# Keys' sums of squares as a product with a matrix of ones, and five rotary-and-plain score products in place of six

## The reference, cut to what matters

```python
q = (rms_norm(c_q, cq_g) @ w_uq).reshape(b_, t_, MLA_HEADS, QK_HEAD)
ckv = rms_norm(c_kv, ckv_g)
k_nope = (ckv @ w_uk).reshape(b_, t_, MLA_HEADS, QK_NOPE)
v = (ckv @ w_uv).reshape(b_, t_, MLA_HEADS, V_HEAD)
k_r = jnp.broadcast_to(k_rope[:, :, None, :], (b_, t_, MLA_HEADS, QK_ROPE))
k = jnp.concatenate([k_nope, k_r], axis=-1)
q = rms_norm(q, qn_g)
k = rms_norm(k, kn_g)
q = jnp.concatenate([q[..., :QK_NOPE], apply_rope(q[..., QK_NOPE:], cos, sin)], axis=-1)
k = jnp.concatenate([k[..., :QK_NOPE], apply_rope(k[..., QK_NOPE:], cos, sin)], axis=-1)
o = causal_block_attention(q, k, v)
```

## Time and profile before

| | us |
|---|---|
| median of three runs | 1754.62 |
| lowest, highest | 1753.0, 1754.93 |
| the profiled execution | 1751.97 |
| its span, first to last instruction | 1750.2 |
| TensorE busy in it | 1734.3 (99%) |
| VectorE busy | 813.8 (46%) |
| ScalarE busy | 467.3 (27%) |
| GpSimd busy | 1183.7 (68%) |

### The profile page before, as it was taken

How to read it: one execution, slowest core, us unless ns; L and a number is a source line. 1 busy time by engine, 2 the same in 40 slices (tenths; PEclk the granted TensorE clock), 3 DMA queues, 4 the chain that set the end, 5 groups by cost and what they waited for, 6 DMA issues and landing times.

```text
span 1750.2 us, 32871 instructions
## 1 busy us (share of the span) xinstructions
PE 1734.3 (99%) x12264; PEld 1626.1 (93%) x12264; DVE 813.8 (46%) x1373; ACT 467.3 (27%) x843; POOL 1183.7 (68%) x1365
## 2 busy tenths in 40 slices
PE   7999999999999999999999999999999999999999
PEld 7999999999999999999999999989998888888887
DVE  7755546455555452212347546464555554422221
ACT  4423223242323331101134232332323233311110
POOL 7754746374798777777766647473847988777773
PEclk9999999999999999999999999999999999999999
DMA  4321212122322223222431312222222222422233
GB/s 158 123 96 54 90 59 84 65 74 70 109 84 84 84 96 130 88 96 85 161 112 64 105 56 74 72 84 68 72 77 104 85 93 86 145 88 92 96 121 110
DMA packets 47489, 161.60 MB, mean 92 GB/s; under 512 B 5408, under 2 KB 6816, under 8 KB 47136
## 3 DMA queue, kind: packets, MB, share of 16 engines
q1 hardware_dynamic: 41328, 146.56, 24.6%
q10 hardware_dynamic: 6112, 14.39, 2.2%
HBM read 152.27 MB, written 10.81 MB: 93 GB/s over the span
## 4 chain that ended last, share of the span: by engine, by line
PE 96%; DVE 2%; ACT 1%; issue 0%; ACTq 0%; DVEq 0%
PE slots L508 83%; PE slots L566 4%; PE slots L599 3%; PE slots L542 2%; PE slots L660 2%; PE slots L584 1%; PE slots L551 1%; DVE h_lo L1099 1%; DVE branch_lo L1111 1%; DVE h_tile L1175 0%; PE slots L701 0%; DVE spare L1120 0%; PE slots L569 0%; ACT cq_hi L849 0%; DVE early L1165 0%
## 5 line engine op out<-in xcount | busy, mean ns | idle before, releaser
L420 POOL TENSOR_TENSOR w_lo<-w_raw,w_hi 128x256 fp32r<-128x256 f32 x1004 | 828.4, 855 | 20.9
L415 POOL TENSOR_SCALAR w_hi<-w_raw 128x1024 fp32r<-128x1024 f32 x251 | 284.0, 1131 | 388.1 <-PE slots L508 380.7
L508 PE MATMUL slots<-h_hi,w_hi 128*128 128x264 f32 (+1 forms) x2112 | 522.8, 311 | 0.6
L508 PE MATMUL slots<-h_lo,w_hi 128*128 128x264 f32 (+1 forms) x2112 | 515.9, 308 | 0.0
L508 PE MATMUL slots<-h_hi,w_lo 128*128 128x264 f32 (+1 forms) x2112 | 515.1, 308 | 0.0
L508 PEld LDWEIGHTS slots<-h_hi,w_hi 128*128 128x128 f32 x2112 | 342.7, 188 | 22.9 <-issue 3.9
L508 PEld LDWEIGHTS slots<-h_hi,w_lo 128*128 128x128 f32 x2112 | 342.0, 188 | 19.1
L508 PEld LDWEIGHTS slots<-h_lo,w_hi 128*128 128x128 f32 x2112 | 342.0, 188 | 17.6
L508 PE MATMUL slots<-branch_hi,w_hi 128*128 128x264 f32 (+1 forms) x576 | 144.0, 313 | 9.6 <-DVE branch_lo L1111 8.9
L508 PE MATMUL slots<-branch_lo,w_hi 128*128 128x264 f32 (+1 forms) x576 | 142.8, 311 | 0.0
L508 PE MATMUL slots<-branch_hi,w_lo 128*128 128x264 f32 (+1 forms) x576 | 142.4, 311 | 0.0
(11 more groups left out here) (243 smaller groups left out, 2825.0 us busy)
## 6 DMA issues: line engine op xcount, KB each, us to landing
w_raw<-w_units SPq DMA_DIRECT2D x251, 512.0 KB, 3.2
stream<-sc_acc ACTq DMA_DIRECT2D x16, 264.0 KB, 3.0
sc_back<-stream SPq DMA_DIRECT2D x2, 2112.0 KB, 8.7
x_old<-stream SPq DMA_DIRECT2D x16, 264.0 KB, 4.4
stream<-residual_or_merged ACTq DMA_DIRECT2D x16, 264.0 KB, 2.5
ab_raw<-w_units SPq DMA_DIRECT2D x8, 512.0 KB, 4.6
residual_or_merged<-xt ACTq DMA_DIRECT2D x4, 528.0 KB, 7.6
stream<-xt ACTq DMA_DIRECT2D x1, 2112.0 KB, 10.3
```

Source lines behind the costliest of these rows:

```text
L415: pool.tensor_scalar(hi, raw, 1.0, 1.0, ALU.mult, ALU.mult).then_inc(sem("hi_part"), 1)
L420: op = pool.tensor_tensor(lo[:, cols], raw[:, cols], hi[:, cols].bitcast(F32), ALU.subtract)
L508: mm = pe.matmul(out[:, a_, 0:t1 - t0], w(k), x(k)[:, t0:t1], start=(n == 0), stop=(n == 3 * ks - 1))
```

## The change

The sums of squares of the keys no longer go through tokens on partitions. A new `spread_sum` multiplies the squares with a 128x128 matrix of ones, so the sum for each token stands on all partitions at once. DVE adds the rotary key's share (`kr_sum`, made once a layer in the same way), ACT takes the root and DVE the reciprocal, both now on 128x528 for each head. The two `spread` products, the ten diagonals and the ten `token_sums` of the keys are gone. The scaled rotary key is now written on all partitions, and `kr_hi` is no longer blank on its other half; the new tile `qr_both` holds for each head the hi part of its rotary queries on its own half and the lo part on the other half. One product of `qr_both` with `kr_hi` is then the sum of hi by hi and lo by hi, and the sixth product is left out. In CQ, the units kr and q1 change places, `stat_q` comes ahead of `rot`, and DVE's work on q1 moves behind `h_lo` of the last tile. In ATT, `rot` stands behind four steps of fill instead of ahead of it.

```diff
-FILLS = (2, 12, 5, 5, 6, 6, 7, 2, 6, 6, 7, 7, 6)
+FILLS = (4, 1, 9, 5, 5, 6, 6, 7, 2, 6, 6, 7, 7, 6)
...
+            def spread_sum(out, squares):
+
+                for a_ in range(2):
+                    mm = pe.matmul(out[:, a_, 0:HALF], ones[0:squares.shape[0], :],
+                                   squares[:, a_ * HALF:(a_ + 1) * HALF], start=True, stop=True)
+                return mm
...
-                             (qn_lo[:, h, :], kn_hi[:, h, :]), (qr_hi, kr_hi[:, h, :]),
-                             (qr_hi, kr_lo[:, h, :]), (qr_lo, kr_hi[:, h, :])]
+                             (qn_lo[:, h, :], kn_hi[:, h, :]), (qr_both[:, h, :], kr_hi[:, h, :]),
+                             (qr_both[:, h, :], kr_lo[:, h, :])]
...
-                out = free("CQ", l, 0, "stat_kr")
-                token_sums(out, [kr_sq[0:ROPE]]).then_inc(sem("cq_mm"), 1)
-
+                out = free("CQ", l, 0, "sum_kr")
+                spread_sum(out, kr_sq[0:ROPE]).then_inc(sem("cq_mm"), 1)
+                out = free("CQ", l, 0, "stat_q")
+                pe.wait_ge(*at("q_lat_summed", l, 0, 2))
+                token_sums(out, [q_lat_sq[0]]).then_inc(sem("cq_mm"), 1)
...
+                    for h in range(2):
+                        out = free("ATT", l, p, f"sum_k{h}")
+                        pe.wait_ge(*at("k_squared", l, p, h + 1))
+                        spread_sum(out, ct[h]).then_inc(sem("att_mm"), 1)
...
                     fill(FILLS[0])
+                    out = free("ATT", l, p, "rot")
+                    pe.wait_ge(*was_read("ATT", l, p, "qr"))
...
-                    pe.wait_ge(*at("qr_lo", l, p, 1))
+                    pe.wait_ge(*at("qr_lo", l, p, 2))
...
+                    for h in range(2):
+                        act.wait_ge(*was_read("ATT", l, p, f"sum_k{h}"))
+                        act.activation(ct[4 + h][:], ct[4 + h][:], ACT.Sqrt, bias=eps, scale=1.0 / QK).then_inc(
+                            sem("k_rms"), 1)
...
+                    for h in range(2):
+                        act.wait_ge(*at("kr_scaled", l, p, h + 1))
+                        act.activation(kr_hi[:, h, :], ct[4 + h][:], ACT.Copy).then_inc(sem("krp_hi"), 1)
+                    act.wait_ge(*at("qr_full", l, p, 1))
                     for h in range(2):
                         rows = slice(ROPE * h, ROPE * h + ROPE)
-                        act.activation(kr_hi[rows, h, :], spare[1][rows], ACT.Copy).then_inc(sem("krp_hi"), 1)
-                    act.wait_ge(*at("qr_full", l, p, 1))
-                    act.activation(qr_hi[:], ct[7][:], ACT.Copy).then_inc(sem("qr_hi"), 1)
+                        act.activation(qr_both[rows, h, :], ct[7][rows], ACT.Copy).then_inc(sem("qr_hi"), 1)
...
+                dve.wait_ge(*ready("CQ", l, 0, "sum_kr"))
+                dve.tensor_copy(halves(kr_sum), slot(slot_of("CQ", "sum_kr"))).then_inc(freed("CQ", "sum_kr"), 1)
...
                     for h in range(2):
-                        diagonal(ct[4 + h], k_inv, h, "k_diag")
+                        dve.wait_ge(*ready("ATT", l, p, f"sum_k{h}"))
+                        if h == 0:
+                            dve.wait_ge(*was_read("NORM", l, 0, "spread"))
+                        dve.tensor_tensor(halves(ct[4 + h][:]), slot(slot_of("ATT", f"sum_k{h}")), halves(kr_sum),
+                                          ALU.add).then_inc(freed("ATT", f"sum_k{h}"), 1)
+
+                    def k_inverse(h):
+
+                        dve.wait_ge(*at("k_rms", l, p, h + 1))
+                        dve.reciprocal(ct[4 + h][:], ct[4 + h][:]).then_inc(sem("k_rinv"), 1)
+
                     for g in range(2):
+                        k_inverse(g)
...
-                        dve.tensor_tensor(halves(ct[2 + h][:]), halves(ct[2 + h][:]), spread, ALU.mult).then_inc(
+                        dve.wait_ge(*at("k_rinv", l, p, h + 1))
+                        dve.tensor_tensor(ct[2 + h][:], ct[2 + h][:], ct[4 + h][:], ALU.mult).then_inc(
                             sem("k_full"), 1)
-                        dve.tensor_tensor(halves(spare[1][rows]), halves(kr_full[rows]), spread[rows],
-                                          ALU.mult).then_inc(freed("ATT", f"spread_k{h}"), 1)
+                        dve.wait_ge(*at("k_full", l, p, h + 1))
+                        dve.tensor_tensor(ct[4 + h][:], kr_full, ct[4 + h][:], ALU.mult).then_inc(
+                            sem("kr_scaled"), 1)
...
-                    dve.wait_ge(*at("qr_hi", l, p, 1))
-                    lo_part(qr_lo[:], ct[7][:], qr_hi[:], "qr_lo")
+                    for h in range(2):
+                        rows = slice(ROPE * h, ROPE * h + ROPE)
+                        other = slice(ROPE * (1 - h), ROPE * (1 - h) + ROPE)
+                        dve.wait_ge(*at("qr_hi", l, p, h + 1))
+                        lo_part(qr_both[other, h, :], ct[7][rows], qr_both[rows, h, :], "qr_lo")
```

More of the change, by code:

```diff
@@ L216, in build @@
         ones = sb("ones", [P, P])
-        lane_consts = sb("lane_consts", [P, 2 + 4 * NTOK])
+        lane_consts = sb("lane_consts", [P, 2 + 2 * NTOK])
         eps, zero = (lane_consts[:, n:n + 1] for n in range(2))
-        kr_stat, x_floor, x_rinv_sq, q_floor = (lane_consts[:, 2 + n * NTOK:2 + (n + 1) * NTOK] for n in range(4))
+        x_floor, q_floor = (lane_consts[:, 2 + n * NTOK:2 + (n + 1) * NTOK] for n in range(2))
         token = sb("token", [P, 16])
@@ L239, in build @@
             kn_hi, kn_lo = a("kn_hi", [P, 2, T]), a("kn_lo", [P, 2, T])
-            qr_hi, qr_lo = a("qr_hi", [P, T]), a("qr_lo", [P, T])
+            qr_both = a("qr_hi_and_lo", [P, 2, T])
             kr_hi, kr_lo = a("kr_hi", [P, 2, T]), a("kr_lo", [P, 2, T])
@@ L566, in scores @@
                         mm = pe.matmul(bank[:, 0:k1 - k0], q[:, q0:q0 + nq], k[:, k0:k1], start=(m == 0),
-                                       stop=(m == 5 and not masked))
+                                       stop=(m == 4 and not masked))
                     if masked:
@@ L692, in _ @@
                             tiles(cq_hi), tiles(cq_lo), KQ).then_inc(sem("att_mm"), 1)
-                    for h in range(2):
-                        out = free("ATT", l, p, f"spread_k{h}")
-                        spread(out, ct[4 + h], lambda t: at("k_diag", l, p, h * NTOK + t + 1)).then_inc(sem("att_mm"), 1)
-                    out = free("ATT", l, p, "rot")
-                    pe.wait_ge(*was_read("ATT", l, p, "qr"))
-                    for a_ in range(2):
-                        mm = pe.matmul(out[:, a_, 0:HALF], rotate, ct[7][:, a_ * HALF:(a_ + 1) * HALF],
-                                       start=True, stop=True)
-                    mm.then_inc(sem("att_mm"), 1)
                     filled = [0]
@@ L721, in _ @@
                     fill(FILLS[0])
+                    out = free("ATT", l, p, "rot")
+                    pe.wait_ge(*was_read("ATT", l, p, "qr"))
+                    for a_ in range(2):
+                        mm = pe.matmul(out[:, a_, 0:HALF], rotate, ct[7][:, a_ * HALF:(a_ + 1) * HALF],
+                                       start=True, stop=True)
+                    mm.then_inc(sem("att_mm"), 1)
+                    fill(FILLS[1])
                     stat = free("ATT", l, p, "stat_q")
@@ L737, in _ @@
                         scores(l, p, n // 5, n % 5)
-                        fill(FILLS[n + 2])
+                        fill(FILLS[n + 3])
                         if n == 5:
@@ L741, in _ @@
                         turn(l, p, n // 5, n % 5)
-                    fill(FILLS[12])
+                    fill(FILLS[13])
                     attend(l, p, 1)
@@ L861, in _ @@
                     h_upper(k)
-                q_latent(1)
+                if l > 0:
+                    act.wait_ge(sem("stored"), l * (16 * KT))
+                act.wait_ge(*ready("CQ", l, 0, "kr"))
+                act.activation(halves(kr_gained[:]), slot(slot_of("CQ", "kr")), ACT.Identity, bias=zero,
+                               scale=hparam(l, KR_G)).then_inc(sem("kr_gained"), 1)
+                act.activation(halves(kr_sq), slot(slot_of("CQ", "kr")), ACT.Square).then_inc(freed("CQ", "kr"), 1)
                 act.wait_ge(*at("kv_ms", l, 0, 1))
@@ L1247, in _ @@
                     other = slice(ROPE * (1 - h), ROPE * (1 - h) + ROPE)
-                    for part in (kr_hi, kr_lo):
-                        dve.memset(part[other, h, :].bitcast(F32), 0.0).then_inc(sem("kr_blank"), 1)
+                    dve.memset(kr_lo[other, h, :].bitcast(F32), 0.0).then_inc(sem("kr_blank"), 1)
                 with dve.Fori(0, PAIRS) as p:
@@ L1602 @@
         kr = w_in[:, K_ROPE:K_ROPE + ROPE]
-        units += [cols(w_in, C_KV, n) for n in range(KV)] + [cols(w_in, C_Q, n) for n in range(KQ - 1)]
-        units += [cols(np.concatenate([kr, kr], 1), 0, 0), cols(w_in, C_Q, KQ - 1)]
+        units += [cols(w_in, C_KV, n) for n in range(KV)] + [cols(w_in, C_Q, 0)]
```

(1 more changed line is left out.)

113 lines of the change are left out of this document (35 added, 78 removed), and 8 rows, old and new, of tables (SIGNALS, TILES).

## The result

The changed kernel took 1768.81 us (median of four runs, 1766.49 to 1771.25), the kernel before 1754.6 us beside it. The ratio is 1.0083, with a 95% interval of 1.0066 to 1.0100. I had predicted 1735 us and a range that ended at 1750 us.

The account below looks back on a forecast made before the run. PE, busy 99% of the span, was taken to bound the kernel. Savings of 14.3 + 12.2 = 26.5 us, less 5.6 and 1.5 of waits, gave 19.4 off 1751.97; plus 2.65 to the median, 1735 us, range 1726 to 1750.

Parts of the forecast that it names:

- The sums: PE in each pair: ten sums over tokens go, one costly change between product kinds comes; net 1.79 us, 14.3 in eight.
- The sixth product: Scores on PE: one of six equal products goes, saving one sixth of 73.5 us, 12.2 us (12.1 to 12.4).
- The gain arrived in time for `rot`: DVE's gain of the rotary queries ends at 171.0, PE wants it at 171.9: covered by 0.9 us.
- The wait at the scores: PE waits for DVE's `qr_lo` at the scores, 0.7 us a pair, 5.6 in eight; bounds none to 2.2 a pair.
- the waits slow the clock too: Rival: each pair's wait at the scores brings a half-clock stretch, adding 13.6 us: 1749 us, or 1745; chance 0.15.
- the three signs of being wrong: Reciprocal over 4 us, PE waiting at `rot` for the gain, or the granted clock falling within the pairs.
- 1.5 in my sum: CQ: `rot` no longer fills PE's wait for the sum of the queries; 0.75 us lost a layer, 1.5 in all (0 to 2.6).
- The half-clock term: Layer 1, behind CQ's wait: clock at 0.57 for four us, 1.7 us lost already before; the sum left it unchanged.
- Slower: Rival: the reciprocal makes eight passes, 4.5 us; PE waits 3.8 us a pair, 30.4 in all: 1760 us; chance 0.12.
- the 4.15 us that I had worked out: Reciprocal time on DVE from which the "Slower" rival decides: the wait eats 3.1 us a pair; 7.6 ns an element.
- No wait: Rival: PE never waits at the scores, through a cheap reciprocal or SBUF operations without traffic: 1728 to 1730 us; chance 0.22.
- The change does not save what it says: Rival: something that stays, such as weight loads, sets the distance of PE's products; 1753 to 1756 us; chance 0.06.

Follow-up runs that it names:

- e4: The changed kernel with six score products as before, so the keys' sums alone: 1753.44 us, 0.9998 of the kernel before.
- e2: The kernel before with five score products in place of six, sums over tokens as before: 1742.43 us, ratio 0.9939.
- f4: The changed kernel with four more fill steps ahead of the scores, `rot` of CQ in slot 0 and RG's first two units' slots exchanged: 1730.17 us, ratio 0.9870.
- h1: The kernel before with two idle reciprocals (528 and 352 columns) on DVE in each pair, ahead of the last lo part: 1785.69 us, ratio 1.0188.
- h2: The kernel before with two idle reciprocals (528 and 130 columns) on DVE in each pair, ahead of the last lo part: 1771.83 us, ratio 1.0104.
- f2: The changed kernel with two more fill steps ahead of the scores, taken from behind the third and fourth score product: 1748.52 us, ratio 0.9972.
- f3: The changed kernel with `rot` of CQ in slot 0 and RG's first two units' slots exchanged: 1760.95 us, 1.0042 of the kernel before.
- g3: f4 with six score products in place of five, so the keys' sums without their waits: 1737.75 us, ratio 0.9908.

## Why the prediction was wrong, point by point

**The PE side was right.** The sums: 1.79 us a pair predicted, 1.88 measured (e4). The sixth product: 12.2 predicted, 11.1 measured (e2). Both without waits: 3.32 predicted, 3.39 in the second pair (f4). The gain arrived in time for `rot`, as I had said.

**The wait at the scores was sized at 0.7 us and is 2.6: the step that failed.** Count from the pair's start, 153.72 in my sum and 157.31 in the trace. PE ended its fill at 30.7 (187.65 + 0.40), predicted 30.9. The gain of the rotary queries ended at 18.0 (175.33), predicted 17.3: from start to start the two reciprocals took 3.37 and 3.36 us and not 2.9, 0.9 in all, the additions took 0.2 more, and some 0.4 came back at the two `qn_lo` and the gain. The four multiplications ended at 23.0 (180.29), predicted 21.3: another 1.0, as they took 5.0 and not 4.0. The last lo part ended at 33.0 (190.34), predicted 31.5. So DVE was 1.5 later, PE 0.2 earlier, and the hand-over took 0.34 (190.34 to 190.68) where I had 0.1: 1.9 us, the difference of 0.7 and 2.6. My upper bound was 2.2 us a pair, so the bounds missed as well, by little.

The group of the reciprocal (count, busy us, mean ns, idle before):

```profile
L1266 DVE RECIPROCAL early<-early 128x528 f32<-128x528 f32 x16 | 55.2, 3448 | 1.0
L1284 DVE TENSOR_TENSOR early<-early 128x528 f32<-128x528 f32 x16 | 19.7, 1234 | 0.0
L1287 DVE TENSOR_TENSOR early<-residual_or_merged,early 128x528 f32<-128x528 f32 x16 | 20.5, 1279 | 0.6
```

The slope from ten elements to 528 is (3448 - 202) / 518 = 6.3 ns; h1 has 6.25 between 352 and 528 columns (2.35 and 3.45 us), and 130 columns in h2 took 0.97 us, on the same line. The small rows had 4.2 to 5.7: a slope over ten elements is a poor guide to one over 500. The Trainium skill, "VectorE: DVE Perf Modes", section "First, the fixed hardware budget", gives the repeat count of 8 that I had read as eight passes; the measured time is below the 4.4 us which that makes (I had written 4.5 for 8 x 1.0 x 528 ns + 0.14 us). For the multiplications I had the right row, 1.26 us beside POOL, and took 1.0 because POOL has pauses; they ran at 1.23 and 1.28 on average, so the dear end was the price.

**Even the right wait would not have given the time.** 21.0 in place of 5.6 is 15.4 us, that is 1751 us. The other 18 have three causes. (1) The clock: the rival "the waits slow the clock too" was right in kind. I gave it 0.15 with a wait of 0.7 us; at 2.6 us it happens, so one of the three signs of being wrong that I had named, a fall of the granted clock within the pairs, came true, though the reciprocal stayed under 4 us. The runs price it at 8.9 us in the pairs (the changed kernel beside f2; 7.4 to 10 by the other two ways), and h1 shows it apart from the change. (2) The end of CQ and of attention: L648 with 3.2 and L1378 with 1.9 us, and the half clock behind them; the same two slots were worth 7.9 us in f3 and 8.8 in f4, against 1.5 in my sum. That 1.5 was for another wait, the one for the sum of the queries, which `rot` no longer covers; it grew from 1.0 to 1.7 us, 0.7 in all. For the two new ones I had looked at the order on PE and not at the slot table: `rot` now takes the slot that DVE's last new pass frees, and `av1` the one that RG wants first. (3) The gap of 3.6 us at L666, which no view of the kernel before could show; 1.1 of it went in f3 and is in the 7.9. Together 15.4 + 8.9 + (7.9 - 1.5) + 2.5 = 33.2 us over 1735.3, that is 1768.5; measured are 1768.8. The fit is closer than the terms are known: each is a difference of medians with an interval of some 3 us, and those across chips move by 1.5 us with the runs of the kernel before.

**The half-clock term left as it is.** Wrong too: it came in CQ of both layers. First layer 0 of the kernel before, a stretch over the end of CQ, then that of the changed kernel:

```profile
52.00:60.00 8.00, 8.00 (x66) 7.45 (x65) 7.49 (x15) 3.97 (x6) 6.48 (x8) 1.00 0.92 333
```
```profile
54.00:64.00 10.00, 7.63 (x42) 7.13 (x43) 7.31 (x13) 1.77 (x4) 9.53 (x13) 0.66 0.79 277
```

**The rivals.** "Slower" had the right sign with a mechanism that holds in part: a dear reciprocal on DVE's chain. It did not need to pass the 4.15 us that I had worked out, because waits also cost clock, which that point left out. "No wait" fell. "The change does not save what it says" fell: g3 and e2 show both savings.

## What to carry to other kernels

Where a change moves work from an engine that never waits to one that is on the path to it for a moment, the question is not the engine's share but its free time at that one handshake; add up every duration of that chain at its dear end (here the reciprocals and the multiplications both came out there or beyond), and see who is late. Two edits that each fit into that free time need not fit together, so price them together, and then shift the covering work so that the counts at all other handshakes stay. When the order of tiles changes, read the slot table for who frees each slot, and do it once for the seams between stages as well.
